# The first recurrent head on raw input, and a buffer of its own for the seventh branch gate

## What is computed

```
x = x + 1/2 SwiGLU_1(RMSNorm(x))
u = RMSNorm(x);  P = u @ w_in     -> lru_x, lru_gate, ssd_z, ssd_xBC, ssd_dt, gate logits gA, gB
A: xc = conv4(lru_x); RG-LRU scan h; (gelu(lru_gate) * h) @ w_br_lru
B: Mamba-2 SSD scan of conv4(ssd_xBC), 4 groups; silu(z) gate, grouped RMSNorm; @ w_br_ssd
x = x + (sigmoid(gA) * A + sigmoid(gB) * B) @ w_out
x = x + 1/2 SwiGLU_2(RMSNorm(x));  final RMSNorm
```

## Time and profile before

| | |
|---|---|
| median of three runs | 1844.07 us |
| the profiled execution | 1844.38 us |
| its span, first to last instruction | 1841.6 us |
| PE busy | 1825.9 us (99%), 12597 instructions |
| DVE busy | 1100.5 us (60%) |
| ACT busy | 660.4 us (36%) |
| POOL busy | 130.1 us (7%) |
| DMA | 185.09 MB, mean 101 GB/s |

### The profile page before, as it was taken

How to read it: one execution, slowest core, us unless ns; L and a number is a source line. 1 busy time by engine, 2 the same in 40 slices (tenths; PEclk the granted TensorE clock), 3 DMA queues, 4 the chain that set the end, 5 groups by cost and what they waited for, 6 DMA issues and landing times. The chain is left out here.

```text
span 1841.6 us, 31210 instructions
## 1 busy us (share of the span) xinstructions
PE 1825.9 (99%) x12597; PEld 1780.6 (97%) x12597; DVE 1100.5 (60%) x1354; ACT 660.4 (36%) x878; POOL 130.1 (7%) x258
## 2 busy tenths in 40 slices
PE   8999999999999999999999999999999999999998
PEld 8999999999999999999989989999999999999998
DVE  6443343345787875787787887877754433442444
ACT  5221332123577752344244235233342212221224
POOL 4000000000002210111101101000200000000000
PEclk9999999999999999999999999999999999999999
DMA  5222222222422253353444335336622222222222
GB/s 151 77 71 72 77 76 72 79 69 65 144 64 71 73 144 107 112 175 93 121 141 129 108 109 168 103 104 225 197 69 80 68 80 69 80 70 78 74 63 91
DMA packets 273102, 185.09 MB, mean 101 GB/s; under 512 B 7340, under 2 KB 260468, under 8 KB 272768
## 3 DMA queue, kind: packets, MB, share of 16 engines
q1 hardware_dynamic: 239984, 129.52, 24.6%
q0 software_dynamic: 10240, 35.86, 6.2%
q10 hardware_dynamic: 22800, 18.62, 3.1%
HBM read 161.43 MB, written 22.53 MB: 100 GB/s over the span
## 5 line engine op out<-in xcount | busy, mean ns | idle before, releaser
L1543 DVE TENSOR_TENSOR w_lo<-w_raw,w_hi 128x1024 fp32r<-128x1024 f32 x240 | 293.9, 1224 | 464.0 <-ACT w_hi L1046 462.6
L662 PE MATMUL pu<-act_hi,w_hi 128*128 128x320 f32 x1940 | 452.6, 314 | 2.0 <-DVE w_lo L1543 1.3
L662 PE MATMUL pu<-act_lo,w_hi 128*128 128x320 f32 x1940 | 443.0, 309 | 0.1
L662 PE MATMUL pu<-act_hi,w_lo 128*128 128x320 f32 x1940 | 442.4, 309 | 0.0
L1046 ACT ACTIVATE w_hi<-w_raw 128x1024 fp32r<-128x1024 f32 x240 | 253.7, 1057 | 515.7 <-PE pu L662 509.3
L662 PEld LDWEIGHTS pu<-act_hi,w_hi 128*128 128x128 f32 x1940 | 323.9, 188 | 15.4 <-issue 11.6
L662 PE MATMUL pu<-x_hi,w_hi 128*128 128x320 f32 x1440 | 328.8, 310 | 1.0 <-DVE w_lo L1543 0.5
L662 PE MATMUL pu<-x_lo,w_hi 128*128 128x320 f32 x1440 | 328.3, 309 | 0.0
L662 PE MATMUL pu<-x_hi,w_lo 128*128 128x320 f32 x1440 | 328.1, 309 | 0.0
L662 PEld LDWEIGHTS pu<-act_lo,w_hi 128*128 128x128 f32 x1940 | 324.9, 188 | 1.5 <-DVE act_lo L1588 0.7
L662 PEld LDWEIGHTS pu<-act_hi,w_lo 128*128 128x128 f32 x1940 | 325.0, 188 | 0.0
(11 more groups left out here) (343 smaller groups left out, 1881.2 us busy)
## 6 DMA issues: line engine op xcount, KB each, us to landing
w_raw<-in_ffn_w_up_dram SPq DMA_DIRECT2D x87, 512.0 KB, 3.8
w_raw<-in_w_in_dram SPq DMA_DIRECT2D x73, 512.0 KB, 3.9
w_raw<-in_ffn_w_down_dram SPq DMA_DIRECT2D x32, 512.0 KB, 3.8
da_rep<-e_spill POOLq DMA_DIRECT2D x20, 512.0 KB, 4.2
w_raw<-in_w_br_ssd_dram SPq DMA_DIRECT2D x16, 512.0 KB, 3.8
w_raw<-in_ffn_w_down_dram SPq DMA_DIRECT2D x16, 384.0 KB, 3.4
gate_spill<-gbuf ACTq DMA_DIRECT2D x17, 320.0 KB, 2.7
merged<-gate_spill POOLq DMA_DIRECT2D x8, 640.0 KB, 5.7
```

The costliest lines, as they stand in the source:

```text
L662: ins = pe.matmul(dst[:, h, :], w[:, side, c, :], a[:, k, h * HALF:(h + 1) * HALF], start=(at == 0), stop=(at == n - 1))
L1543: dve.tensor_tensor(w_lo[:, side, :, :], w_raw[:, side, :, :], w_hi[:, side, :, :].bitcast(F32), ALU.subtract).then_inc(s["w_lo_done"], 1)
```

## The change

- Head 0's gate input also runs on raw input, and its filler is gone. DVE scales its output (`scale_raw(O_LRU + 1)`) ahead of head 0's convolution.
- The gates of head 0 stand behind seven input tiles of unit (1, 0), 42 products, instead of four. That unit waits for each normalised tile.
- The weight cut for unit (1, 0) moves, on ACT to behind the sixth normalised tile, on DVE to behind the first scaling.
- ACT's tanh frees gl0's output; the addition of 1 that DVE made there is folded into the product with bl0.
- gl6 gets a buffer of its own (`gl_next`, another part of `h0_t`). Its fetch and gl7's are issued before gl5's gate; gl6's gate stands ahead of the norm's root on ACT and ahead of its steps on DVE.

```diff
@@ -293,6 +293,7 @@
...
         gl_tanh = lmat[:, 0:NT, :].rearrange("p h l -> p (h l)")
+        gl_next = h0_t[:, 1, 0:NT, :].rearrange("p b n -> p (b n)")
@@ -761,11 +762,6 @@
...

-            def keep_busy(n):
-
-                for _ in range(n):
-                    pe.transpose(pn[0][:, 1, 0:P], ident[:, :], ident[:, :])
-
@@ -803,15 +799,13 @@
...
             ins.then_inc(s["dt_p"], 1)
-            unit(U_LRU + 1, O_LRU + 1, 2, 2, 0, act_hi, act_lo, ready=("xh_done", "xl_done", XH_MIX, 0),
-                 amid={4: lambda: keep_busy(5), 5: lambda: keep_busy(5)})
-            keep_busy(16)
+            unit(U_LRU + 1, O_LRU + 1, 2, 2, 0, x_hi, x_lo)
...

-            unit(U_LRU, O_LRU, 2, 2, 1, act_hi, act_lo, amid={3: first_gates})
+            unit(U_LRU, O_LRU, 2, 2, 1, act_hi, act_lo, ready=("xh_done", "xl_done", XH_MIX, 0), amid={6: first_gates})
@@ -1173,8 +1167,12 @@
...
             act.wait_ge(s["raw_v"], 1)
-            act.activation(halves(gl_buf[0]), out(O_GL), ACT.Tanh, scale=0.5, bias=v(V_BG)).then_inc(s["gl_th"], 1)
-            for k in range(3, KT):
+            act.wait_ge(s["out_free"], O_GL)
+            act.activation(halves(gl_buf[0]), out(O_GL), ACT.Tanh, scale=0.5, bias=v(V_BG)).then_inc(s["out_free"], 1)
+            for k in range(3, 6):
+                norm_cut(k)
+            take(U_LRU, O_LRU, 2, 2, 0)
+            for k in range(6, KT):
@@ -1189,9 +1187,10 @@
...

-                take(U_LRU, O_LRU, 2, 2, j)
...
                     act.wait_ge(s["raw_v"], 2)
+                else:
+                    take(U_LRU, O_LRU, 2, 2, j)
@@ -1201,8 +1200,12 @@
...

-                take(U_LRU + 1, O_LRU + 1, 2, 2, j)
-                act.activation(halves(g_2[:, :]), out(O_LRU + 1), ACT.Square).then_inc(s["lru_a"], 1)
+                if first:
+                    act.wait_ge(s["raw_v"], 3)
+                    act.activation(halves(g_2[:, :]), out(O_LRU + 1), ACT.Square).then_inc(s["lru_a"], 1)
+                else:
+                    take(U_LRU + 1, O_LRU + 1, 2, 2, j)
+                    act.activation(halves(g_2[:, :]), out(O_LRU + 1), ACT.Square).then_inc(s["lru_a"], 1)
@@ -1233,6 +1236,7 @@
...
             lru_front(0, True)
+            take(U_LRU + 1, O_LRU + 1, 2, 2, 0)
@@ -1295,19 +1299,20 @@
...
                 act.wait_ge(s["fs_mm"], 2 * GROUPS)
+                act.dma_start(gl_next, gate_spill[KT - 2, :, 0:TOK]).then_inc(s["gl_next"], 16)
...

-            def last_gate():
-
-                name = ("gl", KT - 1)
+            def last_gate(m):
+
+                name = ("gl", m)
                 ready_mix(name)
-                act.activation(out(O_AT[name]), out(O_AT[name]), ACT.Tanh, scale=0.5, bias=v(V_BG + KT - 1)).then_inc(s["gl_th"], 1)
+                act.activation(out(O_AT[name]), out(O_AT[name]), ACT.Tanh, scale=0.5, bias=v(V_BG + m)).then_inc(s["gl_th"], 1)
...

-            def last_gate_out():
-
-                freed(("gl", KT - 1))
-                act.dma_start(gate_spill[KT - 1, :, 0:TOK], gl_last).then_inc(s["gs_out"], 16)
+            def last_gate_out(m, gate):
+
+                freed(("gl", m))
+                act.dma_start(gate_spill[m, :, 0:TOK], gate).then_inc(s["gs_out"], 16)
@@ -1461,6 +1466,8 @@
...
                 from_state_copy(1)
+                if g == GROUPS - 1:
+                    fetch_last()
@@ -1470,14 +1477,13 @@
...

-            fetch_branch(LAST_UNITS[0][1])
-            fetch_last()
+            last_gate(KT - 2)
             norm_rstd(GROUPS + 1, 0.25 / 512)
-            fill(LAST_UNITS[:1])
-            last_gate()
+            last_gate_out(KT - 2, gl_next)
+            last_gate(KT - 1)
...
                 if q == 2:
-                    last_gate_out()
+                    last_gate_out(KT - 1, gl_last)
@@ -1742,11 +1748,10 @@
...
             norm_tile(3)
-            dve.wait_ge(s["gl_th"], 1)
-            dve.tensor_scalar(gl_buf[0], gl_buf[0], 1.0, None, ALU.add).then_inc(s["out_free"], 1)
...
             scale_raw(O_LRU)
+            cut_weights(U_LRU + 2, 2, 0)
@@ -1830,7 +1835,8 @@
...

-            lru_front(0)
+            scale_raw(O_LRU + 1)
+            convolve(xc[:, :], 0, 2, 0, O_LRU, V_LCW, KT)
@@ -1880,13 +1886,16 @@
...
                 ready_mix(("gl", m))
-                dve.wait_ge(s["gl_th"], m + 1 - sum(n < m for n in LATE_GATES))
+                dve.wait_ge(s["gl_th"], m - sum(n < m for n in LATE_GATES))
...
                 else:
-                    if m < KT - 1:
+                    if m < KT - 2:
...
                         gate = halves(gbuf[:, :])
+                    elif m == KT - 2:
+                        dve.wait_ge(s["gl_next"], 16)
+                        gate = halves(gl_next)
@@ -1908,7 +1917,10 @@
...
                 dve.wait_ge(s["out_free"], O_AT["gl", m] + 1)
-                dve.tensor_tensor(halves(gl_buf[m]), halves(gl_buf[m]), out(O_AT["bl", m]), ALU.mult).then_inc(s["out_free"], 1)
+                if m:
+                    dve.tensor_tensor(halves(gl_buf[m]), halves(gl_buf[m]), out(O_AT["bl", m]), ALU.mult).then_inc(s["out_free"], 1)
+                else:
+                    stt(halves(gl_buf[m]), halves(gl_buf[m]), 1.0, out(O_AT["bl", m]), ALU.add, ALU.mult).then_inc(s["out_free"], 1)
@@ -2153,7 +2165,8 @@
...

-            norm_scale(GROUPS + 1, 0.25 / 512, amid=lambda: fill(LAST_UNITS[:1]))
+            fill(LAST_UNITS[:1])
+            norm_scale(GROUPS + 1, 0.25 / 512)
...
             def split_last(q):
```

More of the change, by code:

```diff
@@ L148 @@
 dt_v dt_a dt_p after_v da_in0 da_in1 xb_th xb_out z_th ssd_p ssd_a ssd_v bseq
-h0_in0 h0_in1 hs_step old_mm old_cp c_split fs_mm fs_cp ns_mm ns_v hs_out0 hs_out1 hp_mm hp_cp hp_out yz yn_hi_done yn_lo_done br_s gl_th gl_mul gl_out0 gl_out1 gl_in gl_last gs_add gs_out
+h0_in0 h0_in1 hs_step old_mm old_cp c_split fs_mm fs_cp ns_mm ns_v hs_out0 hs_out1 hp_mm hp_cp hp_out yz yn_hi_done yn_lo_done br_s gl_th gl_mul gl_out0 gl_out1 gl_in gl_next gl_last gs_add gs_out
 ma_in0 ma_in1 ma_in2 ma_in3 mg_b mg_v mh_done ml_done reload tail_mm tail_cp tails_out fin_half fin_r fin_sq fin_add fin_g fin_sum fin_a fin_v y_a y_v y_dma""".split()
```

## The result

| | before | after |
|---|---|---|
| median | 1844.09 us (1842.91 to 1845.94, 17 runs) | 1847.85 us (1846.65 to 1848.71, 17 runs) |
| ratio | | 1.0019 [1.0013, 1.0026] |
| span of the profiled execution | 1841.6 us | 1845.6 us |
| PE busy | 1825.9 us, 12597 instructions | 1824.8 us, 12571 instructions |

A forecast was written before the change was run, and what follows sets the result against it. The prediction took TensorE (PE), busy 99% of the span, as the bound. Its terms 3.5 + 2.3 - 1.6 = +4.2 us on the profiled 1844.38 gave 1848.6, or 1848.2 us as a median, range 1845.3 to 1850.9.

The forecast's parts named there:

- Start of unit (1, 0): First head: PE starts this unit at 518.2 instead of 517.28, +0.9 us, after 5.2 us idle.
- The gates and g_t: First head: gates 18 products later (2.6 us) plus the late start (0.9), +3.5 us; new 2.8 us wait before unit (1, 1).
- The clock: PE's clock falls once, after the idle piece before unit (1, 0), costing +2.3 us.
- the nearest row: Kernel's start: transposes at 421 against 272 ns, a third of the time lost, put a clock fall at 1.2 to 2.4 us.
- half speed: Clock at 1.2 instead of 2.4 GHz after the first idle piece would cost 1.7 to 3.4 us.
- the second rival: The clock falls twice, also over the 2.8 us wait for g_t; 1850.5 us, chance 0.17.
- The end: Last group: PE's wait for weights in front of gs7 goes, -1.6 us.
- the clock holds: Rival: no clock fall over the gap before unit (1, 0); 1845.9 us, no measurable change, chance 0.30.
- the end fails: Rival, last group: fetches queue with the state's stores and the wait for w_lo stays; 1849.8 us, chance 0.05.
- The faster one: Rival, first head: DVE convolves by 512.95 and PE goes on without a gap; 1840.7 us, chance 0.03.

The follow-up runs named there:

- gates24: The changed kernel with head 0's gates back behind 24 products; 1843.81 us, ratio 0.9999.
- ahead42: The changed kernel with head 0's four copies and convolution moved ahead of the eighth normalised tile, gates still behind 42 products; 1840.98 us, ratio 0.998.
- head_only: The changed kernel with the end of the last group as before, so the first-head part without gl6's buffer; 1849.3 us, ratio 1.0025.
- end_only: The kernel before with only the change's end, gl6's own buffer and early gate; 1842.37 us, ratio 0.9989.
- before_unfilled: The kernel before with its filler transposes taken out and nothing else; 1843.57 us, ratio 0.9997.
- filled_half: The changed kernel with 20 filler transposes in the idle piece before unit (1, 0); 1849.12 us, ratio 1.0023.
- filled: The changed kernel with 40 filler transposes of the identity in the idle piece before unit (1, 0); 1846.69 us, ratio 1.0013.
- gates24_filled: The changed kernel with head 0's gates behind 24 products and 40 filler transposes before unit (1, 0); 1842.83 us, ratio 0.9998.

## Why the prediction was right, and where it was not

The prediction was 1848.2 us, the result 1847.85. The causes of the loss, the late start and the late gates, were forecast rightly; that the total came so close is luck, since the clock fell twice and not once, and what this added came back by other ways. By its steps:

- **Start of unit (1, 0), +0.9.** Right: 517.86 + 0.22 against 517.28 is +0.8. DVE's wait for w_hi was 1.01 (1.1 forecast), the second scaling began at 516.01, the idle piece was 4.86 us (5.2). The profile names "issue" as what ended it, where I had named xc as the releaser; that xc's first step ends it is read from its row at 516.85.
- **The gates and g_t, +3.5 in all.** Right: 3.5, with a wait of 2.84 (2.8 forecast). `gates24` shows that the place of the gates is the larger part.
- **The clock, +2.3 once.** This is the step that was wrong, in size and in count. A fall cost 1.5 us, within the 1.2 to 2.4 that the nearest row gave and below the 1.7 to 3.4 of half speed. It lasted 3.3 us at 0.53 us a pair, 517.86 to 521.12, where 0.29 is the full pace. And the clock fell twice, which was the second rival; I held the wait of 2.8 us to be short, and it fell there in the changed kernel and, by the mean clock, in nine of eleven runs of `ahead42`. 3.0 us instead of 2.3. The nearest row was also a doubtful one: over the slow transposes of the kernel's start the granted clock reads 1.00, in mid-kernel it shows 0.50. What made those transposes slow no run shows; that their loss bounds the price of a fall was a lucky choice.
- **What the sum left out.** 0.7 us comes back between 540 and 1257 us: PE, being late, no longer waits for ACT there. It covers the error of the clock's term, by luck, so the total (+4.2 forecast, +4.0 between the two traces) is better than its parts.
- **The end, -1.6.** Right by the trace, and 1.5 by the median spans of `head_only` and `end_only` (1.5 and 2.0 by their medians). That the fetches would fit into ACT's idle 4.05 us is shown by their rows.
- **The rivals.** That the clock holds is excluded for the changed kernel by the 0.50 in its rows; that the end fails, by `head_only`. The faster one did not come, since the change leaves the convolution behind the last tiles. `ahead42` is that rival built, and its working held: gates forecast at 519.1 and found at 518.78, unit (1, 1) forecast at 525.1 and found at 524.81 (its trace is 0.44 us ahead of the old one before head 0, so 519.2 and 525.3). That 1840.98 us was measured where 1840.7 was forecast is in part luck: the working had no fall of the clock, and nine of the eleven runs seem to have one; the two without took 1839.09 and 1839.68.

The rule of the Trainium skill on the clock (TensorE: Matmul & The Clock Gate, "What's actually happening": the slow level is the default, activity releases it) agrees with the rows in mid-kernel, 0.50 behind 4.86 us of idling. The same section adds that the moment at which the clock is released at a start is not fixed to the program and varies from run to run. No run here shows that moment; `ahead42`, where one program seems to have held the clock in some runs and lost it in most, is a variation of the same kind in mid-kernel.

**What stays open.** What decides whether a piece of 2.2 to 2.8 us costs the clock was not settled: 2.19 us held in the profile of `before_unfilled`, 2.67 fell in `filled_half`, 2.83 and 2.84 held in the profiles of `ahead42` and `filled`, and the clock fell behind 2.83 and 2.84 in those of `filled_half`, `head_only` and the changed kernel. In the three profiles where a second such wait fell (the changed kernel, `head_only`, `filled_half`), another fall stood some 10 us ahead of it, but the mean clocks of `ahead42` say that it needs none. The three longest executions each of `filled` and `gates24_filled`, at a mean clock of 0.999, are not explained by the clock, nor is the longer time of the last stores in three traces, nor the time outside the span of the kernel before. Of the 0.7 us regained 0.46 has its rows.

## What to carry to other kernels

A unit on raw input is ready earlier, but its lead is worth something only if the next unit can start: with two output buffers, look at what frees the one that the next unit needs, and move that reader ahead of the preparation that nobody waits for yet (here 4.3 us beside `end_only`, where the raw unit without that move lost 5.0 beside the kernel before). Operations that start a long chain through other engines belong as early in PE's program as their input allows; 18 products more in front of them cost 1.7 to 2.6 us and a new wait, which then cost the clock too. Of a bound PE, price a long idle piece (here 4.9 us) as its length plus 1.5 us for the clock; for one of 2.2 to 2.8 us these runs leave open whether the 1.5 comes on top, so take both cases into the range. Before a small difference of medians is read as a gain, compare the spans and the last wait of the bound engine too.

## What the runs showed of the hardware that I had not expected

- A fall of the clock in mid-kernel cost 1.5 us in each of the four traces that show one (7.78 against 6.24 us for 42 products; 8.63 against 7.12; 5.14 against 3.59 for 24 products, 517.52 to 522.66 in `gates24` and 517.98 to 521.57 in `gates24_filled`), whether the idle piece was 4.86, 2.84 or 2.67 us long.
- The granted clock over short stretches shows these falls (0.50), while it reads 1.00 over the slow transposes at the kernel's start.
- The clock may fall while PE works: in `filled_half` two pairs ran at the full pace behind the idle piece, and then, 0.7 us after PE had resumed, those at half the pace began.
- Transposes of the identity (128 x 128, 0.11 us each) keep the clock: with 40 of them in place of 4.4 us of idling it read 1.00 in `filled` and `gates24_filled`.
